# Order of the first loads, of the pieces held in the buffers used once, and of two steps of the second layer's merge, in a two-layer diffusion backbone kernel

## The reference

```python
ml = silu(c) @ w_mod[l] + b_mod[l]                 # 6 modulation vectors; mc from c_ctx
h  = rms_norm(x, norm1_g[l]) * (1 + scale) + shift
p  = h @ w_in[l]                                   # q, k, v, pool, hyena (3x), gates (3x1024)
y  = [neighbourhood_attention, multiscale_pool, hyena(long convolutions)]
m  = sum_n sigmoid(gate_n) * (y_n @ w_branch[l, n])
x  = x + ml[2] * (m @ w_out[l])
h2 = rms_norm(x, norm2_g[l]) * (1 + ml[4]) + ml[3]
# 16 experts, top 2 within one group, router shared by the layers
f  = sum_e gate_e * ((silu(h2 @ w_gate[e]) * (h2 @ w_up[e])) @ w_down[e])
x  = x + ml[5] * f                                 # at the end rms_norm(x, final_g)
```

## Time and profile before

| | us |
|---|---|
| runs, median of 3 | 1522.13 (1521.05 to 1523.75) |
| the profiled execution | 1518.69 |
| its span | 1517.0 |
| PE busy | 1428.8 (94%) |
| DVE busy | 846.4 (56%) |
| ACT busy | 636.2 (42%) |
| POOL busy | 402.4 (27%) |
| mean granted TensorE clock | 0.984 |

### The profile page before, as it was taken

The page is one execution under the profiler, slowest core; times in us unless marked ns, Lnnn a source line. Parts: engine busy times, 40 slices in busy tenths (PEclk is TensorE's granted clock), DMA queues, the critical chain, the costliest instruction groups (busy, mean ns, idle before and its releaser), DMA issues. The chain is left out here.

```text
span 1517.0 us, 20465 instructions
## 1 busy us (share of the span) xinstructions
PE 1428.8 (94%) x8088; PEld 1065.8 (70%) x8088; DVE 846.4 (56%) x1291; ACT 636.2 (42%) x865; POOL 402.4 (27%) x366
## 2 busy tenths in 40 slices
PE   6999999899999997899999998999999997999987
PEld 2688788557778874688888863797979995444434
DVE  7625466664223347899999976565863555211112
ACT  3432322364223325578878755542274443110102
POOL 1445434201333530111111013474215570000000
PEclk9999999999999998999999999999999999999998
DMA  9522212565434553899999997252306677799993
GB/s 361 154 85 87 84 56 66 197 249 205 166 135 134 186 220 131 303 406 409 419 411 418 402 352 288 86 173 84 105 22 227 237 267 285 309 421 421 422 420 158
DMA packets 117185, 362.76 MB, mean 239 GB/s; under 512 B 7806, under 2 KB 73664, under 8 KB 86496
## 3 DMA queue, kind: packets, MB, share of 16 engines
q1 hardware_dynamic: 109584, 334.62, 57.9%
q0 software_dynamic: 7360, 26.28, 4.6%
q10 hardware_dynamic: 144, 0.52, 0.1%
HBM read 349.86 MB, written 11.53 MB: 238 GB/s over the span
## 5 line engine op out<-in xcount | busy, mean ns | idle before, releaser
L929 POOL TENSOR_TENSOR w_lo<-ring,w_hi 128x256 fp32r<-128x256 f32 (+1 forms) x300 | 344.2, 1179 | 511.0 <-ACT w_hi L2018 460.0
L1135 PE MATMUL bank<-h_hi,w_hi 128*128 128x512 f32 (+1 forms) x768 | 270.7, 352 | 11.2 <-ACT mix L2071 3.9
L1137 PE MATMUL bank<-h_lo,w_hi 128*128 128x512 f32 (+1 forms) x768 | 262.4, 342 | 0.0
L1136 PE MATMUL bank<-h_hi,w_lo 128*128 128x512 f32 (+1 forms) x768 | 262.4, 342 | 0.0
L1135 PEld LDWEIGHTS bank<-h_hi,w_hi 128*128 128x128 f32 x768 | 146.2, 190 | 38.1 <-issue 9.2
L1136 PEld LDWEIGHTS bank<-h_hi,w_lo 128*128 128x128 f32 x768 | 146.3, 190 | 17.4 <-issue 1.7
L1137 PEld LDWEIGHTS bank<-h_lo,w_hi 128*128 128x128 f32 x768 | 146.2, 190 | 16.6
L1135 PE MATMUL bank<-w_hi,h_hi 128*128 128x512 f32 (+1 forms) x384 | 140.2, 365 | 7.1 <-DVE h_lo L3023 3.1
L2018 ACT ACTIVATE w_hi<-ring 128x1024 fp32r<-128x1024 f32 x120 | 125.5, 1054 | 43.9 <-PE bank L1135 29.8
L1137 PE MATMUL bank<-w_lo,h_hi 128*128 128x512 f32 (+1 forms) x384 | 136.9, 356 | 0.0
L1136 PE MATMUL bank<-w_hi,h_lo 128*128 128x512 f32 (+1 forms) x384 | 136.8, 356 | 0.0
(11 more groups left out here) (403 smaller groups left out, 2874.3 us busy)
## 6 DMA issues: line engine op xcount, KB each, us to landing
ring<-in_w_in SPq DMA_DIRECT2D x52, 1024.0 KB, 5.3
mix<-in_w_gate_e SPq DMA_DIRECT2D x40, 1024.0 KB, 7.7
ring<-in_w_up_e SPq DMA_DIRECT2D x38, 1024.0 KB, 7.7
mix<-in_w_down_e SPq DMA_DIRECT2D x28, 1024.0 KB, 8.1
ring<-in_w_mod SPq DMA_DIRECT2D x19, 1024.0 KB, 7.0
ring<-in_w_down_e SPq DMA_DIRECT2D x19, 1024.0 KB, 7.2
operands_plain<-in_w_up_e SPq DMA_DIRECT2D x18, 1024.0 KB, 13.3
operands_plain<-in_w_mod SPq DMA_DIRECT2D x13, 1024.0 KB, 11.4
```

The costliest lines, as they stand in the source:

```text
L929: last = pool.tensor_tensor(w_lo[:, slot, k:k + n], rview(raw, 8)[:, k:k + n, x * P:(x + 1) * P], w_hi[:, slot, k:k + n].bitcast(F32), ALU ...
L1135: first = mm(dst, stat[0], mov[0], start=start, stop=False)
L1136: mm(dst, stat[1], mov[0], start=False, stop=False)
L1137: return first, mm(dst, stat[0], mov[1], start=False, stop=stop)
```

## The change

Opening: all five pieces beside the ring are asked for ahead of the first projection weights, and the small tables behind the second ones. Second layer: the four places hold the pieces 15, 3, 7 and 6; a list `turns` gives the order of the requests, and the semaphores are counted in this order; the copies of the token rows wait until piece 7 has been used. branch_in(0, 1) is called ahead of the loop. In take_tiles the lead of the tile 16 + at_start comes behind its copy.

```diff
-        once = {1: area(15360, 2048), 2: area(13312, 2048), 3: ahead[:, 0:2048], 7: area(11264, 2048)}
+        once = {15: area(15360, 2048), 3: area(13312, 2048), 7: ahead[:, 0:2048], 6: area(11264, 2048)}
...
+        turns = [[*range(EXP_C)], [0, 15, 3, 7, 1, 2, 4, 5, *range(8, 15), 16, 17, 6, *range(18, EXP_C)]]
+
+        def turn(l, c):
+            return turns[l].index(c)
...
-            return c // (1 + l) % len(x_full)
+            return turn(l, c) // (1 + l) % len(x_full)
...
-                elif c < 3:
+                elif c in (0, 15, 3):
                     sp.wait_ge(a_o[l], len(units_of[l]))
-                elif c == 3:
+                elif c == 7:
                     sp.wait_ge(g_t[l], 3 * DK * l + PRE[l])
-                elif c == 7:
+                elif c == 6:
                     sp.wait_ge(t_pe[l], 8 * l + 2 * (tcols(l) // P))
...
-                    if 2 * len(x_full) <= c:
-                        sp.wait_ge(x_full[piece_sem(l, c)], landed_to(l, c - 2 * len(x_full)))
+                if l and 2 * len(x_full) <= turn(l, c):
+                    sp.wait_ge(x_full[piece_sem(l, c)], landed_to(l, turns[l][turn(l, c) - 2 * len(x_full)]))
...
                     filter_transforms(l)
-                    for k in BESIDE[:2] if l == 0 else ():
+                    for k in BESIDE if l == 0 else ():
                         piece_beside(k)
-                if l == 0 and at == lo + RS + 1:
-                    for k in BESIDE[2:]:
-                        piece_beside(k)
-                if at == at_of[("in", l, 1)]:
+                if at == at_of[("in", l, 2 - l)]:
                     tables(l)
...
-                    expert_load(l, once_behind.index(i))
+                    expert_load(l, turns[l][once_behind.index(i)])
...
-                for c in [4, 5, 6, *range(8, 18), 7, *range(18, EXP_C)] if l else range(EXP_C):
+                for c in turns[l][len(once_behind) * l:]:
                     expert_load(l, c)
...
                     for g in range(done[0], done[0] + n):
-                        if g < 24:
+                        if g == 16 + at_start:
+                            pass
+                        elif g < 24:
                             lead_in(g + AHEAD + 1)
...
+                        if g == 16 + at_start < 24:
+                            lead_in(g + AHEAD + 1)
...
                 parts_in(0)
                 if l:
                     branch_in(0, 0)
+                    branch_in(0, 1)
...
-                        if l and m == 2:
+                        if l and m == 2 and n:
                             branch_in(n, 1)
...
                         tanh(s)
+                        if l and s == 0:
+                            act.wait_ge(x_u, EXP_C * l + gate_up_chunk(l, 0, 7) + 1)
                         for j in range(T // P if l and s == 0 else 0):
                             A(rows_hi[:, j, :], htok[:, j, :], ACT.Copy).then_inc(x_hh, 1)
```

More of the change, by code:

```diff
@@ L665, in landed_to @@
             late = sum(len(late_places[j]) for j in range(DK) if late_sem(j) == piece_sem(l, c)) if l else 0
-            return 16 * (beside + late + EXP_C // n * l + (c // n + 1 if l == 0 else 2 * (c // 2 // n + 1)))
+            return 16 * (beside + late + EXP_C // n * l + (c // n + 1 if l == 0 else 2 * (turn(l, c) // 2 // n + 1)))
         def full_at(idx):
```

## The result

The changed kernel takes 1526.11 us (median of 12 executions, 1522.26 to 1535.68) against 1520.29 us for the kernel before beside it (12 executions, 1516.16 to 1526.05): ratio 1.0043, 95% interval 1.0029 to 1.0056. That is +6.5 us (4.4 to 8.5), slower by more than the 0.2% that this kernel's measurement can tell. It lies in the range of the prediction, but not in its likeliest case.

What follows compares the result with a forecast made beforehand. Expert-piece loading was taken to bound the end, with DMA full from 1312 to 1488 us. Terms +0.7 - 0.9 - 0.9 - 1.2 - 1.8 - 2.5 + 4.7 + 1.7 + 1.7 = +1.5 on 1522.1 gave 1523.6 us, range 1518.5 to 1528.0.

Steps and rivals of the forecast that it cites:

- likeliest case: Whole kernel: no measurable difference, 1523.6 us, within 3 us either way; gains eaten by the token rows' wait; chance 0.5.
- opening: First layer's start: first projection weights land at 38.3, so mod_rows runs at 41.7 instead of 40.98; +0.7 us.
- first and second take: take_tiles in both layers: TensorE's holes at 160.07 and 1025.29 each shrink by 0.9 us with the order turned.
- clock behind the second take: TensorE from 1025.3 to 1028.2: with a shorter hole ahead, the half-clock stretch gives half of itself back, -1.2 us.
- merge: branch 4 to seventh gate: Second layer: the hoisted split lets branch 4 start 1.75 us earlier and the gate follow; -1.8 us.
- clock behind the gate: Seventh gate: the hole ahead grows to 3.0 us and a half-clock stretch follows, +1.7 us.
- 24th piece: Second layer's expert loading: 24 pieces, not 23, are in by the first pair's end; -2.5 us in the full stretch.
- rows wait: Second layer's experts: token-row copies wait for the last first-pair product, delaying L1730 and the full DMA stretch; +4.7 us.
- clock behind it: One half-clock stretch of 3.3 us behind the 5.3 us hole at the token rows, +1.7 us, bounds 0 and 3.4.
- a chance for the weights to overtake: Opening: with free landing order the weights land where they do now, 1.0 us less, 1522.6 us; chance 0.15.
- The 0.3 us to gain: Opening: all that asking earlier for pieces 5 to 7 can give, from TensorE's load for piece 7 at 39.85.
- slower rival: DMA restart follows the token rows' wait in full, clock falls for two stretches: +4.4 us, 1526.5 us; chance 0.3.

Runs made afterwards that it cites:

- the unchanged kernel: The kernel before, with no edit, timed against itself: ratio 1.0006 (0.9990 to 1.0021).
- the copies alone: The kernel before with only the order of copy and lead in take_tiles turned: ratio 0.9975, -3.8 us.
- The late split: The kernel before with branch_in(0, 1) ahead of the loop and VectorE's split of the second y part moved from m = 1 to m = 3: 0.9986, -2.1 us.
- the hoist alone: The kernel before with only branch_in(0, 1) called ahead of the loop: ratio 0.9982, -2.7 us.
- opening alone: The kernel before with only the change's edit of the opening: ratio 1.0018, +2.7 us.
- the turned opening: The kernel before with the opening's edit, plus ScalarE's spectrum copies and mod_rows ahead of its first two weight copies in layer one: 1.0049, +7.4 us.
- the best kernel: The kernel before with take_tiles' order turned, pieces 15, 3, 2, 7 in the four places, branch_in(0, 1) hoisted, second y split at m = 3: 1512.25 us, 0.9948.

## Why the prediction was right or wrong, step by step

Terms at their places, by the start times ahead of and behind each; the clock only where it fell behind an edited place:

| step | predicted | trace after |
|---|---|---|
| opening | +0.7 | +2.9 |
| first and second take | -0.9, -0.9 | -0.95, -0.95 |
| clock behind the second take | -1.2 | -1.45, as in the unchanged kernel |
| merge: branch 4 to seventh gate | -1.8 | -0.1 |
| clock behind the gate | +1.7 | +1.5, and -1.65 back by 1185 |
| 24th piece | -2.5 | -2.5 at the 31st request |
| rows wait | +4.7 | +4.6 |
| clock behind it | +1.7 | +2.4 |
| sum | +1.5 | +3.8 |

*The number.* That 1526.11 us lies in the range of 1518.5 to 1528 is in part luck. The range was added up on a base of 1522.1 us, from three runs; beside the changed kernel the kernel before took 1520.29. Counted from its base, the high end allows +5.9 us (its own sum, 1526.5 + 1.8, would be 1528.3, so +6.2), and measured were +6.5 by the ratio and +5.8 by the medians. The likeliest case, no measurable difference, did not come.

*Opening: a mis-sized term, the step that failed most.* The mechanism was right: mod_rows stands behind w_hi on ScalarE. "Landing 30.8 + 3 x 2.49 = 38.3" was 1.4 too early. The pieces ahead of them were in at 35.4, as the sum has it (27.8 + 3 x 2.49 = 35.3, from the landings in the trace of before); but the first weights then took 4.2 us instead of 2.5. My reading, not tested by itself, is that they shared the engines with what SyncE had asked for behind them, the small tables above all: dft_z, asked for at 30.74, landed at 42.16, ahead of the second weights, asked for at 23.75 and landed at 42.67. With one piece moved and only another 1 MB piece asked for right behind the weights, the rule "one behind the other" held (33.4). The trace of before had the sign already: there piece 7, with dft_z asked for right behind it, landed 4.05 us behind piece 6, and dft_z ahead of it, at 39.2. The Trainium skill, DMA: Bandwidth & Descriptors, section Queues, rings and completion order, says that completion need not follow the order of issue. The trace agrees, with the landings of dft_z and the second weights; I had weighed it only as a chance for the weights to overtake, not as something that could make them later. The other part, +0.8, I had not counted at all: for GpSimd's w_lo I asked only when the first product needs it, not who runs beside it. I had the right place for a bound ("up to 1 us more") for another reason, and the bound of +2.5 for the whole term was passed by 0.4. The 0.3 us to gain could not show behind the late weights; with ScalarE's order turned, mod_rows came at 40.39, 0.6 earlier than before, of which 0.3 was there already at the spectrum copies (37.64 against 37.91).

*Copies: right, the clock behind them: right by luck.* The holes shrank by 0.95 us in both the changed kernel and the copies alone. The step "So the stretch of 2.9 us at half clock ... gives half of itself back" took a fall that the one trace happened to have for one that the hole always brings: seven of nine traces with the same hole have none. A trace without it sits 1.45 us better there, edited or not. Leaving this row out, the places sum to +5.2 us, which lies in the measured 4.4 to 8.5, where +3.8 does not.

*Merge: the step "the split stands behind that of branch_in(0, 0) ... so nothing queued behind it is late" failed.* VectorE's mix step at 1137.81 was indeed not late. But the split of the second y part, which used to run alone at 1139.73, now met GpSimd. Before, ScalarE had made ctx_hi just ahead of the w_hi copy; hoisted, the w_hi copy and so GpSimd's w_lo came earlier against VectorE's work. I had noted a slow w_lo step beside VectorE's late split as something to gain, and did not ask what that step would meet next. As the hole ahead of branch 4 stayed, so did the request behind it and the gate. The late split in its experiment gives 1.9 us at branch 4 and at the gate, about my term of 1.8. The Trainium skill, SBUF — State Buffer, section SBUF: two separate sides, says that VectorE and GpSimd exclude each other for a whole instruction on a shared pair of ports, the later one waiting. The trace agrees: 3.46 us for a step of 1.22 that began 0.02 behind one of 2.39.

*The clock behind the gate: right in size, without effect.* +1.5, but the merge's holes of 0.65 and 0.83 us at 1182 and 1185 in the trace of before are gone in the changed kernel: TensorE, late, found VectorE's results ready. I had counted no such room. Nor does the fall belong to the hoist alone: it stands at the gate in four of the five traces with the hoist and in four of the nine without; in four more of the nine, that of before among them, it stands behind branch 4, where the gate's wait for the weights takes it up.

*Places and rows wait: right.* Two requests together at 1290, five instead of four ahead of the restart, the rows behind the last product, a hole of 5.17 us. The full stretch followed: the restart at +10.55 is the +3.6 from further up, 4.6 and 2.4; the 31st request in order lands 8.0 us late, 2.5 less. The clock was down for two stretches of 3.4 us, not the one of 3.3 I took, the first 0.9 us of it in the hole; my bound of 3.4 us of loss held.

So the slower rival described the outcome: the restart followed the rows wait in full, the clock fell for two stretches, and the merge gave nothing. The last came out by another way than it said: not -1.8 and +1.7, but -0.1, +1.5 and -1.65. Its opening was too cheap by 2.2, of which its own upper end included 1.8.

What the table leaves: the two traces differ by 8.7, not 3.8. Of the other 4.9 us, 2.4 arise between 162 and 1025, where nothing was edited, and 1.5 at 1222, where the clock fell; the unchanged kernel against itself shows the like (3.3 us by 926). Another 1.7 arise inside the full stretch, where the last transfer lands 9.7 us late and not 8.0, and a fall at 1490, which of the two only the trace of before has, takes 1.5 off again; the rest is under 1 us. Twelve executions differ by 6.5 us, interval from 4.4. Their mean granted clock is 0.979, against 0.982 in 29 executions of the kernel before. Among the 88 executions of the kernel before that ran beside the experiments, 0.001 less goes with 0.7 to 1.0 us more, so by this estimate some 2.4 to 3.5 of the 6.5 us go with the clock. Whether TensorE's later start in the opening makes it stand at half clock more often elsewhere, or twelve executions happened to, is open: opening alone (+2.7) speaks against it; the turned opening (+7.4, with 4.1 at 48 us) and the mean clock of both (0.981 each, 12 and 8 executions) speak for it.

## What to carry to other kernels

Before a place is given to another buffer, list what is written there next and choose the tenant whose last use that writer already waits for; here one index was worth about 7 us. When work is moved earlier or later, look at which of VectorE and GpSimd runs beside it: a split moved by two steps brought branch 4 the 1.9 us earlier that the hoist alone had not. A load that is put back has a certain room: 2.6 us late the weights cost 0.2, 8.9 us late they cost 2.9. Find the instruction in whose program order the delayed one stands, and count how far it is away. And look at a stretch at half clock in a second trace of the same kernel before counting on it: here the first trace had one at the second take and the second had none.

## What was not expected of the hardware

The same hole, 3.23 us ahead of the seventh gate and ended by the same GpSimd step, was followed by a granted clock of 1.00 in the best kernel (window above), and by 0.62 in the kernel with the hoist and the late split:

```profile
1152.00:1156.00 4.00, 4.00 (x23) 4.00 (x24) 0.00 (x0) 1.06 (x1) 4.00 (x2) 0.62 1.00 375
```

So the length of a hole alone does not say whether the clock falls behind it. The 5.17 us hole went with a fall in all three kernels that have it, and the eleven others have none at that place; the 2.34 us hole at the second take went with one in two of nine traces, the 1.4 us hole there in none of five. And one kernel against itself differs by 3.3 us in start times between such falls, and by 4.6 at the end, which is more than most parts of this change are worth.
